# One convolution tile less on TensorE, one more on ScalarE with GpSimd, statistics after the z columns, residual loaded by rows

## What is computed

```python
proj = h @ w_in + b_in                       # 1024 -> 3 * 2048
val, glu_gate, z = jnp.split(proj, 3, axis=-1)
u = val * jax.nn.sigmoid(glu_gate)
u = causal_depthwise_conv(u, conv_w, 31 taps) + conv_b    # 2048 channels
u = jax.nn.silu(layer_norm(u, norm_g, norm_b))            # statistics over the 2048 channels
u = u * jax.nn.silu(z)
y = u @ w_out + b_out                        # 2048 -> 1024
h = layer_norm(alpha * h + y, ln_g, ln_b)
```

## Time and profile before

| | |
|---|---|
| median of 3 runs | 899.72 us (899.52 to 900.37) |
| the profiled execution's own time | 898.75 us |
| its span, first to last instruction | 897.0 us |
| TensorE busy | 860.2 us (96%) |
| VectorE busy | 607.1 us (68%) |
| GpSimd busy | 486.4 us (54%) |
| ScalarE busy | 399.5 us (45%) |
| mean granted TensorE clock | 0.982 of full |

### The profile page before, as it was taken

One profiled execution on the slowest core, in us unless ns is written; L12 is line 12 of the kernel. 1 busy time (PEld: TensorE's weight loads), 2 busy tenths in 40 slices (PEclk: granted clock), 3 DMA queues, 4 the chain that ended last, 5 costly groups with the idle time before them and its releaser, 6 DMA issues.

```text
span 897.0 us, 11802 instructions
## 1 busy us (share of the span) xinstructions
PE 860.2 (96%) x4059; PEld 714.5 (80%) x4059; DVE 607.1 (68%) x1077; ACT 399.5 (45%) x694; POOL 486.4 (54%) x272
## 2 busy tenths in 40 slices
PE   5999999999999989799899999999999999989996
PEld 4888888888888767588698788878988888978885
DVE  2899999999999538420842292039778779768207
ACT  3655444436653447621332344146555565545110
POOL 3578888877995462384654437424324424126443
PEclk7999999999999979899999999999999999999999
DMA  6242333320044325243043334321232320223212
GB/s 205 77 119 76 104 96 95 95 75 0 1 118 118 94 71 188 73 134 98 1 139 109 95 93 130 80 68 41 61 82 70 82 80 13 71 94 141 94 48 95
DMA packets 111351, 78.99 MB, mean 88 GB/s; under 512 B 14023, under 2 KB 98093, under 8 KB 111277
## 3 DMA queue, kind: packets, MB, share of 16 engines
q1 hardware_dynamic: 111308, 78.44, 29.1%
HBM read 71.87 MB, written 2.10 MB: 82 GB/s over the span
## 4 chain that ended last, share of the span: by engine, by line
PE 88%; DVE 4%; issue 2%; POOL 2%; ACT 1%; DMA 1%; SPq 0%; POOLq 0%; DVEq 0%; ACTq 0%
PE bank L1421 83%; PE bank L1686 2%; DMA x_in<-in_x_dram 1%; PE bank L1675 1%; PE bank L1676 1%; DVE bank L1195 1%; DVE g_lo L1199 1%; POOL vsum_odd L616 1%; POOL w_lo L561 1%; DVE res L1245 0%; ACT w_hi L719 0%; PE bank L1432 0%; PE bank L1500 0%; DVE pt_lo L1360 0%; DVE fg_lo L1405 0%
## 5 line engine op out<-in xcount | busy, mean ns | idle before, releaser
L561 POOL TENSOR_TENSOR w_lo<-w_raw,w_hi 128x1024 fp32r<-128x1024 f32 x103 | 253.7, 2472 | 205.6 <-ACT w_hi L719 179.8
L1105 DVE SCALAR_TENSOR_TENSOR bank<-u,conv_w,bank 128x512 f32<-128x512 f32 x348 | 233.5, 750 | 0.9
L1421 PE MATMUL bank<-xt_hi,w_lo 128*128 128x512 f32 x384 | 154.6, 403 | 1.4 <-DVE xt_lo L1044 1.4
L719 ACT ACTIVATE w_hi<-w_raw 128x1024 fp32r<-128x1024 f32 x103 | 107.0, 1053 | 104.8 <-PE bank L1421 52.0
L1421 PE MATMUL bank<-xt_lo,w_hi 128*128 128x512 f32 x384 | 153.4, 399 | 0.0
L1421 PE MATMUL bank<-xt_hi,w_hi 128*128 128x512 f32 x384 | 153.1, 399 | 0.0
L1421 PEld LDWEIGHTS bank<-xt_hi,w_lo 128*128 128x128 f32 x384 | 73.7, 192 | 19.4 <-DVE xt_lo L1044 1.8
L1421 PEld LDWEIGHTS bank<-xt_lo,w_hi 128*128 128x128 f32 x384 | 73.5, 191 | 17.5 <-issue 0.5
L1421 PEld LDWEIGHTS bank<-xt_hi,w_hi 128*128 128x128 f32 x384 | 73.5, 191 | 17.4
L588 POOL TENSOR_TENSOR acc<-acc,tap_product 128x512 f32<-128x512 f32 x60 | 77.9, 1298 | 8.5 <-ACT tap_product L753 1.6
L669 POOL TENSOR_TENSOR bundle_lo<-bundle_raw,bundle_hi 128x1024 fp32r<-128x1024 f32 (+1 forms) x16 | 47.1, 2961 | 62.3 <-ACT bundle_hi L917 62.3
(11 more groups left out here) (198 smaller groups left out, 1815.4 us busy)
## 6 DMA issues: line engine op xcount, KB each, us to landing
w_raw<-in_a_w_in_dram SPq DMA_DIRECT2D x48, 512.0 KB, 3.7
w_raw<-in_b_w_in_dram SPq DMA_DIRECT2D x20, 512.0 KB, 3.6
w_raw<-in_a_w_out_dram SPq DMA_DIRECT2D x16, 512.0 KB, 3.7
w_raw<-in_b_w_out_dram SPq DMA_DIRECT2D x16, 512.0 KB, 3.5
bundle_raw<-in_b_w_uq_dram SPq DMA_DIRECT2D x16, 256.0 KB, 3.8
x_in<-in_x_dram SPq DMA_DIRECT2D x4, 512.0 KB, 7.0
res<-in_x_dram SPq DMA_DIRECT2D x1, 2048.0 KB, 7.8
bundle_raw<-in_kv_w_uk_dram SPq DMA_DIRECT2D x8, 256.0 KB, 3.0
```

Source lines behind the costliest of these rows:

```text
L561: nc.gpsimd.tensor_tensor(w_lo[slot][:], w_raw[raw][:], w_hi[slot][:].bitcast(F32), ALU.subtract).then_inc(w_lo_ready, 1)
L719: nc.scalar.activation(w_hi[slot][:], w_raw[raw][:], ACT.Copy).then_inc(w_hi_ready, 1)
L1105: nc.vector.scalar_tensor_tensor(out=bank[CONV_BANK[slot]][:] if k < TAPS - 1 else acc[:, t, :], in0=u[:, t, k:k + SEQ], scalar=conv_w[:, ...
L1421: last = nc.tensor.matmul(out_ap, a, b, start=(start and n == 0 and m == 0), stop=(stop and n == len(parts) - 1 and m == 2))
```

## The change

`MATRIX_TILES` becomes tile 13 alone; `SHARED_TILES` becomes tiles 2, 6 and 10; twelve tiles stay with VectorE. The 93 shared taps are dealt out as 4 in each round from round 4 on (48), 16 beside TensorE's convolution, and 3 beside each z column (29, in columns 0 to 9). The mean goes to z column 14; the variance and the spreading go behind column 15. ScalarE keeps z one column later, squares tiles 0 to 7 in its step 15, and 8 to 15 after the last z column is kept. The residual is loaded in four rows and the other rows one by one, each behind a weight chunk, with a semaphore for each.

```diff
-        MATRIX_TILES = (12, 13)
-        MATRIX_BANK = (6, 3)
+        MATRIX_TILES = (13,)
+        MATRIX_BANK = (6,)
         TAP_GROUPS = tuple(range(8 * g, min(8 * g + 8, TAPS)) for g in range(4))
-        SHARED_TILES = (3, 9)
+        SHARED_TILES = (2, 6, 10)
...
-        PAIR_SHARE, MATRIX_SHARE, Z_SHARE = 3, 20, 2
+        PAIR_SHARE, MATRIX_SHARE, Z_SHARE = 4, 16, 3
...
-        MEAN_AT, VAR_AT, SPREAD_AT = 11, 14, 15
-        SQUARES = {14: range(0, 4), 15: range(4, 9), OUT0 - Z0: range(9, CT)}
+        MEAN_AT = 14
+        SQUARES = {CT - 1: range(0, CT)}
...
             sp.wait_ge(w_used, OUT0)
-            sp.dma_start(res[:], x_rows).then_inc(res_landed, 16)
-            sp.dma_start(ln_rows[:, 0, :], ln_g[0:1, :].broadcast_to([P, D_MODEL])).then_inc(res_landed, 16)
-            sp.dma_start(ln_rows[:, 1, :], ln_b[0:1, :].broadcast_to([P, D_MODEL])).then_inc(res_landed, 16)
-            sp.dma_start(ln_rows[:, 2, :], a_b_out.broadcast_to([P, D_MODEL])).then_inc(res_landed, 16)
             for n in range(SLOTS, CT):
                 load_output(OUT0, n, w_out_a)
+                r = n - SLOTS - 1
+                if n == SLOTS:
+                    sp.dma_start(ln_rows[:, 2, :], a_b_out.broadcast_to([P, D_MODEL])).then_inc(bias_landed, 16)
+                elif r < RT:
+                    sp.dma_start(res[:, r, :], x_rows[:, r, :]).then_inc(res_landed[r], 16)
+                elif r == RT:
+                    sp.dma_start(ln_rows[:, 0, :], ln_g[0:1, :].broadcast_to([P, D_MODEL])).then_inc(ln_a_landed, 16)
+                elif r == RT + 1:
+                    sp.dma_start(ln_rows[:, 1, :], ln_b[0:1, :].broadcast_to([P, D_MODEL])).then_inc(ln_a_landed, 16)
...
                 if i == 0:
                     glu(CT - 1, (CT - 1) % 2)
                     for g in range(len(TAP_GROUPS)):
-                        conv_matrices(1, g)
                         for n in matrix_taps(g):
                             add_product(n)
                 for n in z_taps(i):
                     add_product(n)
-                add_odd_squares(SQUARES.get(i, ()))
-            split_lo(OUT0, OUT0 % 2, OUT0 % SLOTS)
-            add_odd_squares(SQUARES[CT])
+                if i in SQUARES:
+                    split_lo(OUT0, OUT0 % 2, OUT0 % SLOTS)
+                    add_odd_squares(range(0, 8))
+                    split_lo(OUT0 + 1, (OUT0 + 1) % 2, (OUT0 + 1) % SLOTS)
+                    add_odd_squares(range(8, CT))
...
             for k in range(CT):
                 c = OUT0 + k
-                if k > 0:
+                if k > 1:
                     split_lo(c, c % 2, c % SLOTS)
-                if 6 <= k < 6 + RT:
-                    r = k - 6
+                if 7 <= k < 7 + RT:
+                    r = k - 7
+                    if r == 0:
+                        pool.wait_ge(bias_landed, 16)
                     pool.wait_ge(res_scaled, r + 1)
...
                 if i == 0:
                     keep_value_gate(CT - 1, (CT - 1) % ROUND)
                     for g in range(len(TAP_GROUPS)):
-                        conv_matrices(1, g)
                         for n in matrix_taps(g):
                             tap_times_u(n)
                     keep_conv(0)
-                if i == 2:
-                    keep_conv(1)
-                for t in SQUARES.get(i, ()):
-                    square(t)
-                if i >= 3:
-                    keep_z(i - 3)
+                if i >= 4:
+                    keep_z(i - 4)
+                if i in SQUARES:
+                    output_split(0)
+                    keep_z(CT - 4)
+                    for t in range(0, 8):
+                        square(t)
+                    output_split(1)
+                    keep_z(CT - 3)
+                    output_split(2)
+                    keep_z(CT - 2)
+                    keep_z(CT - 1)
+                    for t in range(8, CT):
+                        square(t)
                 for n in z_taps(i):
                     tap_times_u(n)
-            output_split(0)
-            for t in SQUARES[CT]:
-                square(t)
-            keep_z(CT - 3)
-            output_split(1)
             act.wait_ge(rstd_cols_ready, 1)
...
-            keep_z(CT - 2)
-            output_split(2)
             for t in range(CT + 1):
-                if t == 3:
-                    keep_z(CT - 1)
...
-                if 5 <= k < 5 + RT:
-                    r = k - 5
-                    act.wait_ge(res_landed, 64)
+                if 6 <= k < 6 + RT:
+                    r = k - 6
+                    act.wait_ge(res_landed[r], 16)
...
             dve.wait_ge(res_ready, RT)
+            dve.wait_ge(ln_a_landed, 32)
...
-                if i == VAR_AT:
-
-                    pe.wait_ge(vsum_done, CT // 2)
...
-                if i == SPREAD_AT:
-                    spread_rstd()
-                if i == 3:
-                    pe.wait_ge(pe_conv_kept, len(MATRIX_TILES))
                 columns(Z0 + i, i % SLOTS, i % 4, Z0 + i - 3, xt_hi, xt_lo)
-            if SPREAD_AT == CT:
-                spread_rstd()
+            pe.wait_ge(vsum_done, CT // 2)
+            pe.wait_ge(vsum_odd_done, CT // 2)
+            for b in range(RT):
+                for n, part in enumerate((vsum, vsum_odd)):
+                    last = nc.tensor.matmul(bank[7][:, b:b + 1], part[:, b * P:(b + 1) * P], ones[:, 0:1],
+                                            start=n == 0, stop=n == 1)
+            last.then_inc(var_done, 1)
+            spread_rstd()
```

More of the change, by code:

```diff
@@ L304, in trunk_kernel @@
         cu_hi_ready, cu_lo_ready = sem("cu_hi_ready"), sem("cu_lo_ready")
-        diag_used, pe_conv_done, pe_conv_kept = sem("diag_used"), sem("pe_conv_done"), sem("pe_conv_kept")
+        pe_conv_done, pe_conv_kept = sem("pe_conv_done"), sem("pe_conv_kept")
         product_ready, product_added = sem("product_ready"), sem("product_added")
@@ L314, in trunk_kernel @@
             sem("scaled"), sem("silu_done"), sem("gated"), sem("g_hi_ready"), sem("g_lo_ready"))
-        res_landed, res_scaled, res_ready = sem("res_landed"), sem("res_scaled"), sem("res_ready")
+        res_landed = [sem(f"res_landed{r}") for r in range(RT)]
+        bias_landed, ln_a_landed = sem("bias_landed"), sem("ln_a_landed")
+        res_scaled, res_ready = sem("res_scaled"), sem("res_ready")
         y_done, y_step, var_row_ready, rstd_row_ready, rstd_step, row_ready = (
@@ L574, in value_gate @@
                 if 2 <= t < 2 + len(TAP_GROUPS):
-                    conv_matrices(0, t - 2)
+                    conv_matrices(t - 2)
                 if t - 2 in MATRIX_TILES:
@@ L589, in add_product, with conv_matrices @@
                                         ).then_inc(product_added, 1)
-            def conv_matrices(m, g):
+            def conv_matrices(g):
                 lo, hi = TAP_GROUPS[g][0], TAP_GROUPS[g][-1] + 1
                 n = hi - lo
[L596 to L600, removed]
+                pool.wait_ge(taps_hi_ready, 1)
+                taps = conv_w_hi[:, MATRIX_TILES[0] * TAPS + lo:MATRIX_TILES[0] * TAPS + hi].bitcast(F32)
                 nc.gpsimd.tensor_tensor(diag_hi[:, lo:hi, :],
@@ L754, in tap_times_u, with conv_matrices @@
                                          ).then_inc(product_ready, 1)
-            def conv_matrices(m, g):
-                if m == 1:
-                    act.wait_ge(diag_used, g + 1)
+            def conv_matrices(g):
                 for k in TAP_GROUPS[g]:
-                    column = MATRIX_TILES[m] * TAPS + k
+                    column = MATRIX_TILES[0] * TAPS + k
                     nc.scalar.activation(
@@ L771, in keep_conv @@
                 t = MATRIX_TILES[m]
-                act.wait_ge(*((diag_used, len(TAP_GROUPS)), (pe_conv_done, 1))[m])
+                act.wait_ge(pe_conv_done, m + 1)
                 nc.scalar.activation(acc[:, t, :], bank[MATRIX_BANK[m]][:], ACT.Identity,
@@ L1464, in convolve @@
                 pe.wait_ge(cu_lo_ready, m + 1)
-                wait(pe, evacuated, 2 * CT if m == 1 else 0)
                 for g, taps in enumerate(TAP_GROUPS):
@@ L1471, in convolve @@
                     last = product(bank[MATRIX_BANK[m]][:], parts, g == 0, g == len(TAP_GROUPS) - 1)
-                    if m == 0:
-                        last.then_inc(diag_used, 1)
-                if m == 1:
-                    last.then_inc(pe_conv_done, 1)
+                last.then_inc(pe_conv_done, 1)
             pe.wait_ge(xt_lo_ready, 2 * RT)
@@ L1493, in _ @@
                     nc.tensor.matmul(bank[7][:], ones[:], csum[:], start=True, stop=True).then_inc(mean_done, 1)
-                if i == VAR_AT:
-                    pe.wait_ge(vsum_done, CT // 2)
-                    pe.wait_ge(vsum_odd_done, CT // 2)
-                    for b in range(RT):
-                        for n, part in enumerate((vsum, vsum_odd)):
```

(13 more changed lines are left out.)

## The result

The changed kernel takes 905.4 us (median of 5 runs, 903.82 to 905.99) against 899.72 for the kernel before: ratio 1.0057, 95% interval 1.0039 to 1.0074. That is slower by 5.7 us; 3.4 had been forecast. The profiled execution took 905.56 us, its span is 903.7.

What follows compares the result with a forecast made beforehand. TensorE is busy 96%, but layer A's mark is the start of chunk 4, set by when the statistics are ready: 375.7 against 372.34, so +3.4 us on the median 899.72 gives 903.1 us, range 898.5 to 907.5.

Steps and rivals of the forecast that it cites:

- Gate columns: A fourth GpSimd add makes rounds 11.55 us instead of 11.15; TensorE first 1.9 us late, gate columns ending 4.0 us late.
- the unstarved 299.0: Time in us at which z column 14 would start if TensorE were never starved.
- z columns: Three adds and a low part take GpSimd 6.48 us against 5.6 a column, so TensorE is starved through column 9.
- 16 taps with one tap 0 are 15 adds, 21.2: GpSimd's adds beside TensorE's convolution: 21.2 us, ending at 226.9, before z column 1's low part at 233.4.
- Mean, variance, scaling: Statistics around the end of z: column 14 at 313.2, variance matmuls 333.9, scaling of tile 0 342.0, chunk 4 at 375.7.
- After chunk 4: The output projection from chunk 4 on: its 3.4 us later start was carried to the end unchanged.
- The loads: Residual in rows and reordered loads: nothing taken for them, bounds 0 and some 4 us.
- Rival 1: Faster: splits run ahead, TensorE isn't starved in gate and z columns; 889.0 us, or 891.3 with VectorE's wait; chance 0.13.
- Rival 2: Slower still: the clock swings to half in the starved z columns, 8 us more, 911 us; chance 0.05.
- Rival 3: No difference: the tail is some 3 us shorter through earlier squares or cheaper adds, 899.7 us; chance 0.10.
- rival 4: A load in the open after chunk 4, 4 us more, 907 us; chance 0.04.
- the 21.7 us: Price of the 93 TensorE matmuls removed between gate columns and z, forecast as given back to starvation and the statistics.

Runs made afterwards that it cites:

- e4_mean12: The changed kernel with the mean at z column 12 instead of 14: 905.54 us against 899.99 for the kernel before, ratio 1.0055.
- e1_loads: The kernel before with only the residual loaded in rows, each load behind a weight chunk: 900.27 us against 899.99, ratio 1.0.
- e8b_left_out: The changed kernel without taps 1 to 30 of shared tile 10 (wrong output), 12 taps beside the convolution: 895.39 us against 899.91, ratio 0.9947.
- e5_under: The changed kernel with statistics under z again: mean at column 12, squares interleaved, variance behind column 15: 894.92 us against 899.71 for the kernel before, ratio 0.9949.
- e2_stats: The kernel before, its tile shares kept, with only the statistics moved behind z as in the changed kernel: 911.05 us against 899.99, ratio 1.0112.
- e3_shares: The kernel before with only the new shares (one tile on TensorE, three shared), statistics and loads as before: 902.31 us against 899.99, ratio 1.0025.
- e6_under15: Changed kernel's shares and loads, statistics under z, mean at column 12, variance ahead of column 15, spreading behind it: 895.35 us against 899.71 for the kernel before, ratio 0.9956.

## Why the prediction was right, and what it mis-sized

**Gate columns: right.** Rounds of 11.55 us were forecast, 11.53 measured; a first wait of 1.9 us at column 12, 1.63 measured. The idle time marked in TensorE's waits adds up to 10.0 us before the mean (14.3 marked "issue" less the 4.64 before chunk 4, and 0.3 marked as GpSimd's), where some 14 were foreseen; but the mean itself came 15.7 us behind the unstarved 299.0 (315.74 - 1.08), so the starvation was not smaller than forecast, only less of it shows as idle time.

**z columns: right in kind, 1.3 us short at one place.** 6.48 us a column was forecast, 6.49 measured. The first 60 us of this profile, which the change does not touch, run later: the glu of round 4 starts at 66.88 where the earlier trace rows have 65.80, 1.08 us. With that taken off, z column 1 had its low part at 234.7 instead of 233.4. The step that failed is "16 taps with one tap 0 are 15 adds, 21.2": the price of an add was right, but GpSimd stands 0.83 us at the change of tile, and 0.44 us once before. ScalarE in the kernel after shows why it stands at the change of tile:

```profile
224.85 0.80 ACT L756 ACTIVATE acc<-u,vec,conv_w 128x512 f32<-128x512 f32 x1
...
227.10 0.72 ACT L760 ACTIVATE tap_product<-u,conv_w 128x512 f32<-128x512 f32 x1 [1.45 <-POOL acc L595]
```

Writing the accumulator does not hold it up, that is done by 225.65. But taps take the two product buffers in turn, and tap 0 takes a turn without using a buffer; so the product of tap 1 goes into the buffer of tap 30 before it, and must wait until GpSimd has added that. ScalarE waits 1.45 us for the add and then GpSimd waits for the product. From the start of the first of these adds to that of the low part of column 1 it took 233.44 - 206.81 = 26.6 us, where 25.3 were counted.

**Mean, variance, scaling: right.** Forecast 313.2, 333.9 and 342.0; less the 1.1 and the 1.3, measured 313.3, 333.8 and 342.1, and chunk 4 at 375.8, where 375.7 was forecast. The standstill after z was to be some 9 us, and was 8.29. e4_mean12 shows that the reason given for the variance (VectorE can't pass tile 10 before square 8) holds, and that the 12 us of slack of VectorE are real: with the mean 10.6 us earlier nothing changes.

**After chunk 4: a term left out.** The sum was carried from chunk 4 to the end as if equal. The windows of TensorE (length, busy, granted clock) for the kernel after say otherwise (the last figures of a row are the DMA share and GB/s):

```profile
378.00:382.00 4.00, 3.78 (x9) 0.50 0.56 179
382.00:390.00 8.00, 8.00 (x31) 0.86 0.76 270
```

and for the kernel before:

```profile
372.00:376.00 4.00, 3.66 (x9) 0.52 0.53 137
376.00:384.00 8.00, 8.00 (x36) 1.00 0.37 128
```

From the start of chunk 4 the clock stays at half for 6.0 us, in the kernel before for 3.5. The 24 matmuls of chunk 4 take 8.40 us instead of 7.28, 1.1 us more; from there the two kernels run alike to the end of the output projection, and layer B gives 0.3 back, which makes 0.8 by the spans (903.7 - 378.22 = 525.5 against 897.0 - 372.34 = 524.7). So 3.4 forecast, 1.3 at the change of tile and 0.8 after chunk 4 make 5.5, against 5.7 measured by the medians. The two profiled executions lie 6.8 apart (905.56 and 898.75): they have the 1.1 us at the start besides, for which the medians leave next to no room.

**The loads: right**, by e1_loads. **Rival 1** (TensorE not starved) fell by the timeline, and e8b_left_out shows what it would have needed: the adds gone. **Rival 2** (the clock swings): z columns 5 to 10 have some 0.66 us of idle before them in 6.5 and keep the full clock. The window of TensorE over them in the kernel after:

```profile
256.00:290.00 34.00, 30.67 (x129) 1.00 0.29 84
```

The Trainium skill's rule (TensorE: Matmul & The Clock Gate, "A second HAM failure mode"), that short idles between groups of matmuls can make the clock swing, was the basis of that rival; here it did not come about. The only column at the low clock in the z stretch is the one after the 4.15 us wait, and GpSimd's pace absorbed it as foreseen: the idle time before columns 2 to 4 is 0.2 us or less, and the low parts keep their 6.5 us. The price of the rival was read too low: at the low clock matmuls start 0.427 us apart (378.79 to 379.21 and on in the kernel after, and the same in the kernel before), not 0.385, so it would have cost some 1.4 us a column and not 0.9. **Rival 3** is out by the runs, and no wait for a load after chunk 4 (**rival 4**) appears among TensorE's waits.

**What the forecast's account of the 21.7 us got wrong in emphasis.** It gave 14.2 of them to starvation and the rest, with 3.4 more, to the statistics, as if the first were lost in any case. The experiments show that a kernel with the same starvation is 4.8 us faster than the kernel before (e5_under), and that the statistics behind z alone cost 11.1 (e2_stats). With the statistics where they were, the new shares lose 2.3 (e3_shares), and there it is VectorE's late sum, with the low clock behind it, that eats the gain; with three constants moved they gain 4.8. The loss of the change lies in the statistics; the starvation only takes away what could have paid for it.

## What to carry to other kernels

Follow an engine that works in written order through the stage that the change touches, instead of reading its share of the span: GpSimd had 54% over the span and 0.96 us of slack in a round of 11.15, so one more add of 1.4 us in each made it the pace of TensorE. Work taken from the bounding engine counts only up to the next point at which it must wait for the others, so ask first what that point waits for, and whether it can stand elsewhere: between e3_shares and e5_under, which differ in little else, lie 7.1 us. A chain of small steps over several engines (mean, squares, variance, scaling) belongs under the last big block of matmuls; moved behind it, it cost 11.1 us here (e2_stats), and an earlier start of its first half gave nothing back (e4_mean12).

## What the runs showed of the hardware

The same 16 one-column matmuls of the variance, from their start to VectorE's instruction behind them, take 3.58 us at the low clock, after TensorE has stood 8.29 us before them, and 1.88 at the full clock, when it comes from z without a gap. The first fence has that instruction of VectorE in the kernel after (the matmuls start at 336.20), the second in e5_under (they start at 326.08):

```profile
339.78 0.16 DVE L1186 TENSOR_SCALAR var_cols<-bank 128x4 f32<-128x4 f32 x1 [5.13 <-PE bank L1499]
```

```profile
327.96 0.16 DVE L1183 TENSOR_SCALAR var_cols<-bank 128x4 f32<-128x4 f32 x1 [8.53 <-PE bank L1498]
```

It is the clock and not the wait that makes the difference: in e6_under15 TensorE waits 1.44 us before them, the granted clock stays at full, and they take 1.96 us (323.18 to 325.14). So this step of the chain costs 1.7 us less where it follows a block of matmuls before the clock has fallen.

What a wait costs at the low clock behind it depends on when in the wait the clock falls. The windows around the wait before chunk 4, first in the kernel before, then in the kernel after:

```profile
366.00:372.00 6.00, 0.21 (x1) 0.75 0.00 0
```

```profile
372.00:378.00 6.00, 1.58 (x7) 0.95 0.00 0
```

In the kernel before TensorE stopped at 366.2, the clock fell at 369.0 and was back at 375.9, so of the 6.8 us at half clock TensorE had work in the last 3.5 (from 372.34). In the kernel after it stopped at 373.6, the clock fell only at 377.4 and was back at 384.3: again 6.8 us at half, but with work in 6.0 of them (from 378.22). The shorter wait, 4.6 us against 6.1, was followed by the longer stretch of slow matmuls. Nor does a wait of one length always do the same: after 4.20 us before z column 1 in e5_under TensorE began at the full clock (0.47 us for the first matmul at 234.27), which fell at 235.4 under the running matmuls and was back at 238.8; after 4.15 us at the same place in the kernel after the clock was already at half when TensorE began at 235.90 (0.77 us for the first matmul) and was back at 240.9. So a difference of a microsecond between two versions can lie in this alone.
